# Projections, state-space mixer and out-projection of a hybrid decoder layer, from two staged programs to one unrolled one

## What is computed

```python
proj = rms_norm(x) @ w_in                       # 1024 x (z 1024, x/B/C 1536, dt 16, u 1024, v 1024)
xbc  = silu(causal_conv4(xbc))                  # split: xs 1024, B 2x128, C 2x128
dt   = softplus(dt + dt_bias); a = -exp(a_log)
y, state = ssd_scan(xs, dt, a, B, C, s0, chunk=128)      # 16 heads, state 128
y    = group_rms_norm((y + d_skip * xs) * silu(z)) * ssm_norm_w
u, v = gelu(u), rms_norm(gelu(v)) * sg_norm_w
y_sg = u * (tril(sg_w) @ v + sg_b)              # 8 heads, chunks of 128 rows
h    = x + concat(y, y_sg) @ w_out              # 2048 -> 1024
g    = rms_norm(h)                              # then top-1 of 4 groups, top-2 of 8 experts
h    = h + sum_k gate_k * (silu(g @ Wg[e]) * (g @ Wu[e])) @ Wd[e]
out  = rms_norm(h)
```

## Time and profile before

| | |
|---|---|
| three runs, us | 1735.78, 1738.29, 1739.23 (median 1738.29) |
| span of the profiled execution | 1732.9 us, 23263 instructions |
| its own device time | not listed apart from the span; the median run is 5.4 us above it |
| busy, share of the span | PE 88%, PEld 68%, DVE 63%, ACT 41%, POOL 25% |
| mean granted TensorE clock | 0.922 |
| HBM read, written | 295.30 MB, 55.31 MB |

### The profile page before, as it was taken

The page is one execution under the profiler, slowest core; times in us unless marked ns, Lnnn a source line. Parts: engine busy times, 40 slices in busy tenths (PEclk is TensorE's granted clock), DMA queues, the critical chain, the costliest instruction groups (busy, mean ns, idle before and its releaser), DMA issues. The chain is left out here.

```text
span 1732.9 us, 23263 instructions
## 1 busy us (share of the span) xinstructions
PE 1517.2 (88%) x7338; PEld 1182.8 (68%) x7338; DVE 1099.1 (63%) x1495; ACT 711.1 (41%) x1014; POOL 437.7 (25%) x323
## 2 busy tenths in 40 slices
PE   5999999999958887779898992899999999999950
PEld 4999998999945544445454222678888888878740
DVE  5014786300147656665654435799999999999947
ACT  6222223322112211222122013677777787777723
POOL 6333333222334212221111000153232322212111
PEclk8999999999978988889898586899999999999985
DMA  4223223232553221122211404899999999999947
GB/s 142 75 78 94 74 87 127 74 98 66 204 176 115 94 95 41 53 94 94 94 59 55 144 29 152 300 395 391 378 381 373 380 379 375 376 372 373 358 176 307
DMA packets 139824, 334.82 MB, mean 193 GB/s; under 512 B 17264, under 2 KB 30352, under 8 KB 138480
## 3 DMA queue, kind: packets, MB, share of 16 engines
q1 hardware_dynamic: 123024, 292.06, 46.5%
q0 software_dynamic: 16768, 42.36, 7.0%
HBM read 295.30 MB, written 55.31 MB: 202 GB/s over the span
## 5 line engine op out<-in xcount | busy, mean ns | idle before, releaser
L59 PE MATMUL bank<-xh,wh 128*128 128x352 f32 x864 | 282.2, 327 | 1.9 <-POOL xl L555 1.9
L61 PE MATMUL bank<-xh,wl 128*128 128x352 f32 x864 | 278.0, 322 | 0.0
L60 PE MATMUL bank<-xl,wh 128*128 128x352 f32 x864 | 278.0, 322 | 0.0
L932 PE MATMUL bank<-w_out_ssm,yT 128*128 128x512 f32 (+1 forms) x288 | 140.4, 650 | 52.3 <-ACT yT L1047 52.3
L1528 ACT CAST wg_h<-wg 128x1024 fp32r<-128x1024 f32 x128 | 135.4, 1058 | 113.2 <-DMA wu<-in_w_up 92.4
L1637 DVE TENSOR_TENSOR wg_l<-wg,wg_h 128x1024 fp32r<-128x1024 f32 x128 | 156.3, 1221 | 25.7 <-ACT wu_h L1529 24.4
L59 PEld LDWEIGHTS bank<-xh,wh 128*128 128x128 f32 x864 | 163.0, 189 | 2.4 <-POOL xl L555 2.0
L60 PEld LDWEIGHTS bank<-xl,wh 128*128 128x128 f32 x864 | 163.4, 189 | 0.0
L61 PEld LDWEIGHTS bank<-xh,wl 128*128 128x128 f32 x864 | 162.7, 188 | 0.0
L451 DVE COPY stage<-bank 128x512 f32<-128x512 f32 x52 | 33.5, 686 | 194.9 <-PE bank L243 194.6
L1638 DVE TENSOR_TENSOR wu_l<-wu,wu_h 128x1024 fp32r<-128x1024 f32 x128 | 155.9, 1218 | 0.0
(11 more groups left out here) (315 smaller groups left out, 2973.9 us busy)
## 6 DMA issues: line engine op xcount, KB each, us to landing
wg<-in_w_gate SPq DMA_DIRECT2D x128, 512.0 KB, 6.3
wu<-in_w_up SPq DMA_DIRECT2D x128, 512.0 KB, 11.8
wd<-in_w_down SPq DMA_DIRECT2D x128, 512.0 KB, 12.3
w<-in_w_in_tiles SPq DMA_DIRECT2D x36, 512.0 KB, 3.3
yy<-scratch_picked SPq DMA_DIRECT2D x8, 1024.0 KB, 12.7
scratch_xb<-stage POOLq DMA_DIRECT2D x10, 512.0 KB, 3.9
xb<-scratch_xb SPq DMA_DIRECT2D x8, 640.0 KB, 7.2
scratch_uT<-feat POOLq DMA_DIRECT2D x8, 528.0 KB, 5.4
```

The lines of the kernel that those rows point to most:

```text
L59: nc.tensor.matmul(acc, lh, rh, start=start, stop=False)
L60: nc.tensor.matmul(acc, lh, rl, start=False, stop=False)
L61: return nc.tensor.matmul(acc, ll, rh, start=False, stop=stop)
L932: last = nc.tensor.matmul(bank[6 + n][0:r2, :], yT[:, k, 0:r2], w_out_ssm[:, k, n * 512:(n + 1) * 512], start=False, stop=(k == KT - 1))
```

## The change

`projections` and `mixer` become one function `front` without loops on any engine. Every SBUF tensor has a hand-given offset in one arena, so that tensors of different phases share bytes. What it does, part by part:

1. **Order of the 36 weight tiles:** first x, B and C (12), then z (8), then eight pairs of one v tile and one u tile. The products themselves (`group`, 24 matmuls for one of three banks) are the same.
2. **dt:** the high and low parts of its weights stand side by side as 32 columns (`w_dt_hl`), so 48 matmuls instead of 72, and they run while the input is still being normalised. What follows is done on 128 partitions x 144 instead of 16 x 1056.
3. **State-space work** of prompt tile i is put between the six groups of v tile i and u tile i (`for i in range(NT)`, lines 589 to 663 of the new file). Its y is scaled, turned, multiplied by `ssm_norm_w` and stored to scratch `yT`.
4. **Sample tile:** its chunk work sits between z tiles. The product of C with an old state becomes 8 matmuls of 4 columns on the state of one sequence (line 647), and one sequence is finished in each of the eight pairs.
5. **Out-projection last:** weights are streamed, 16 slices of 512 KB, three times over (48 slices), each cast by ACT and split by POOL. Three token tiles share a slice: 3 tiles x 2 halves x 3 float32r matmuls of 512 columns.
6. **Spatial gating and routing** are spread over the 16 steps of each group of three tiles: gating in steps 1 to 6, and the norm, turning, router and counts of the three tiles of the group before in steps 0 to 14. Those of the last three tiles come behind the last product.

The cores of it, from the diff (the two old functions are taken out whole):

```diff
-            projections(nc, A, S, C, bank)
-            mixer(nc, A, S, C, bank)
+        front(nc, A, S, C, bank)
...
+    z, xbc, u, v = w[:, :COL_X], w[:, COL_X:COL_DT], w[:, COL_U:COL_U + D], w[:, COL_U + D:]
+    pairs = [part[:, i * P:(i + 1) * P] for i in range(NT) for part in (v, u)]
+    columns = np.concatenate([xbc, z, *pairs], axis=1)
...
+            for i in range(NT):
+                group(qV, 0)
...
+                sums((0, 1))
+                group(qV, 1)
+                    turn_y(i - 1, y)
+                group(qV, 2)
+                sums((2, 3))
+                group(qU, 0)
+                turn(qV)
...
+                group(qU, 1)
...
+                group(qU, 2)
...
...
+            for g in range(3):
+                for k in range(16):
+                    n = 16 * g + k
+                    pe.wait_ge(w_split, W_DONE + n + 1)
+                    for a in range(GROUP):
+                        sh, sl = (yTh[a], yTl[a]) if k < 8 else (ysgh[a], ysgl[a])
+                        for half in range(2):
+                            last = split_product(nc, bank[2 * a + half][0:r, :], (sh[:, k % 8, 0:r], sl[:, k % 8, 0:r]),
+                                                 (woh[n % 3][:, s], wol[n % 3][:, s]), start=(k == 0), stop=(k == 15))
```

More of the change, by code:

```diff
@@ L1 @@
+import math
 from contextlib import ExitStack
@@ L133, in projections @@
[L133 to L140, removed]
@@ new lines, in at, with own @@
+        def at(name, offset, shape, dt=F32):
+            return nc.alloc_sbuf_tensor_at(name, shape, dt, offset=base + offset)
+        used = [SMALL_AT]
+        def own(name, shape, dt=F32):
+            t = at(name, used[0], shape, dt)
+            used[0] += -(-4 * math.prod(shape[1:]) // 32) * 32
+            assert used[0] <= ARENA, (name, used[0])
+            return t
+        xin = [at(f"xin{j}", SEG_AT + 4096 * j, [P, D]) for j in range(3)]
+        xn = [at(f"xn{j}", SEG_AT + 12288 + 4096 * j, [P, D]) for j in range(2)]
@@ new lines, in products, with dt_products @@
+            def products(q):
+                for b in range(NB3):
+                    group(q, b)
+            def dt_products(b):
+                pe.wait_ge(w_split, 1)
+                cols = slice(b * TB, (b + 1) * TB)
+                for k in range(KT):
+                    nc.tensor.matmul(bank[3 + b][0:2 * HEADS, 0:TB], w_dt_hl[:, k, :], xh[:, k, cols], start=(k == 0), stop=False)
+                    last = nc.tensor.matmul(bank[3 + b][0:HEADS, 0:TB], w_dt_hl[:, k, 0:HEADS], xl[:, k, cols], start=False, stop=(k == KT - 1))
+                last.then_inc(dt_psum, 1)
@@ L293, in _ @@
-            products(M_END, M_END - 1, 1)
-            turn(M_END - 2 - (M_V - M_C), M_END - 2, 0)
-            turn(M_END - 1 - (M_V - M_C), M_END - 1, 1)
+                        dt_products(b)
+                        group(0, b)
+            products(1)
+            pe.wait_ge(dt_evicted, NB3)
+            pe.wait_ge(x_scaled, 2 * (NT + 1))
+            for t in range(NT + 1):
+                r = rows_of(t)
+                last = nc.tensor.transpose(bank[6][0:r, 32 * t:32 * t + 32], dt_raw[:, rows(t)], C["ident"][0:32, 0:32])
@@ L416, in _ @@
+            for k in range(15):
+                route_steps(2 * GROUP, k)
         @block.vector
@@ new lines, in count, with route_steps @@
+            def count(t):
+                r = rows_of(t)
+                dve.wait_ge(count_psum, t + 1)
+                wait(dve, counted, t)
+                after(nc.vector.tensor_tensor(S["before"][0:r, t, :], bank[7][0:r, 64:64 + E], run[0:r, :], ALU.add))
+                nc.vector.tensor_tensor(run[:], bank[7][:, 96:96 + E], run[:], ALU.add).then_inc(counted, 1)
+            def route_steps(t0, k):
+                if k == 0:
+                    for t in range(t0, t0 + GROUP):
+                        add_x(t)
+                    norm_h(t0)
+                if k == 1:
+                    norm_h(t0 + 1)
+                if k == 4:
+                    route(t0)
+                if k == 5:
+                    norm_h(t0 + 2)
+                if k == 7:
+                    route(t0 + 1)
+                if k == 8:
+                    count(t0)
+                if k == 10:
+                    route(t0 + 2)
+                if k == 11:
+                    count(t0 + 1)
+                if k == 14:
+                    count(t0 + 2)
```

2122 lines of the change are left out of this document (1156 added, 966 removed).

## The result

The changed kernel takes 1614.33 us (four runs, 1612.51 to 1617.76), the kernel before beside it 1738.7: ratio 0.9292, 95% interval 0.9276 to 0.9309. That is 124 us less, where 152 were forecast: the time lies in the range and 28 us above the point. The profiled execution spans 1613.2 us.

What follows compares the result with a forecast made beforehand. PE was taken to bound the projections, DMA the experts, with the mixer PE with holes. Stage terms put the end of the tail at 906 instead of 1058.6, 152 us less: 1738.3 - 152 = 1586 us, range 1560 to 1645.

Steps and rivals of the forecast that it cites:

- the carried 5.4 us of median over span: Whole kernel: the median of the runs was taken to stay 5.4 us above the profiled span, as before.
- signs of being wrong: Pair above 41 us, group above 90, last count over 50 behind last product, or experts' stage differing by over 5.
- Getting started: Start to the end of the first weight tile: dt's matmuls add 6 us, so it ends at 57.
- x/B/C and z tiles: Weight tiles after the first, with turnings, sample chunk work and 2 us for DVE's dt operations: 242.5 us, to 299.5.
- Pairs: Eight pairs of v and u tiles with state-space work: 39.3 us each at full clock, 314.4 in all, to 614.
- The 0.8 us of stall: In each pair, PE waits 0.8 us for the chain from sums to diagonal products, added to 38.5 us of work.
- rival (b): Pairs have a hole: masks shift by one POOL operation, diagonal products start later; 36 us, 1622 in all; chance 0.16.
- Out-projection: Products 196.5 us, gating, turning, routing, waits of 13, sum 247.5, plus 3.5 for things overlooked: ends at 865.
- Rival (a): DVE and ACT set the out-projection's pace: a group lasts 99 us instead of 84, 45 in all, 1631; chance 0.22.
- Rival (d): Slower than before: straight-line code can't be fed to PE; at 40 ns lost a record, 1784 us; chance 0.04.
- Tail: Last product to last count: three tiles left sharing banks and DVE's chain, 41 us (bounds 33 and 50), to 906.
- experts: What follows the tail: untouched by the change and starting from the same state, so no difference was forecast.

Runs made afterwards that it cites:

- the last run: Changed kernel with 4-column matmuls apart, decay inputs behind masks, other buffer, weight slices first, and weight splits on DVE, behind the additions at group changes: 1578.3 us.
- e1: Kernel before the change, with ACT evicting the turned y ahead of the router's first exponential instead of behind it: 1697.7 us, ratio 0.9783.

## Why the prediction was right in kind and 28 us short

The mechanism is the one that was forecast: PE's idle time fell in sum as counted, and the float32r products took the place of the plain ones. Two terms of the sum were too small, the pairs by 13.6 us and the out-projection by 12.9, and the carried 5.4 us of median over span, too large by 4.3, hid a part of it. Of its own signs of being wrong only one showed, a pair above 41 us: the first, with 50.73, while the others took 38.75 to 40.33. A group of the out-projection took 88 us, and the last count came 39.3 us behind the last product.

**Getting started**, 57 forecast, 60.6 measured. Here executions differ: in kernels with the same code up to this point the second turning of a weight tile's output starts between 82.18 and 86.77 us (85.56 in the profile of the change), with a mean clock of the first 60 us between 0.80 and 0.97. So most of the 3.6 us can be this spread; what dt itself costs was not measured.

**x/B/C and z tiles**, 242.5 forecast, 247 measured (60.6 to 307.6). The waits of over 0.3 us are 2.93 (for ACT's eviction, which stands behind ACT's own work on dt, three table loads of 1.28 us and three activations), 1.18 and 0.55. I had booked 2, and for DVE's share of dt, not for ACT's.

**Pairs**, 314.4 forecast, 328 measured. The sum of PE's work, 38.5, was right to 0.25: 38.75. The 0.8 us of stall that I had booked is in no steady pair. The step that failed is the sentence that, as PE has no holes, I take full clock. PE had no holes and lost the clock in four of seven distances, 6.3 us in all. And the first pair differs from the others: rival (b) came true in this one pair, at 12 us where it said 4.5. What was held against that rival, that DVE gets the port between POOL's two operations, was so in the other pairs (longest mask 4.09 us) and not in this one (9.37), and the low clock came on top.

**Out-projection**, 251 forecast, 263.9 measured. Idle time was right (17.9 for 13 + 3.5), though not where I had it: I had named four at the start for y's split, and it was 6.5 for the store of the state. PE's busy time was not right: 234.5 forecast, 244.7 measured, 239.9 in the last run at a clock of 0.99. (One price was a record's length, 1.95 for the gating, where starts give 1.79 (602.74 - 600.95 in e1); that made the forecast 1.4 us too long, not too short.) So about half of the 10 us is the low clock behind waits, and at most 5 are work that my prices missed; the last run has 3.8 us at a clock of 0.56 too, so the parting is rough.

**Rival (a)**, that DVE and ACT set the pace, was wrong as the pace of the changed kernel, where PE has 17.9 us of idle time in 262.65, and right as a cost: with POOL's splits nearly gone the stage is 15 us shorter, a third of the 45 that it said. **Rival (d)** fell: behind the one slow stretch the records of straight-line code stand 0.16 us apart, as in the loops of before. The Trainium skill, Runtime: NRT & Kernel Launch, section Instruction fetch mechanics, says that the engine's sequencer fetches the next block while it executes the current one; the trace agrees, with the same 0.16 and no extra distance, though it does not show the fetching itself.

**Tail**, 41 forecast, 39.3 measured; **experts**, 674 forecast and 674.4 measured. And the median lies 1.1 us above the span, where I had carried 5.4 over from before: 4 us the other way. The terms together: 3.6 + 4.5 + 13.6 + 12.9 - 1.7 = 32.9, less 4.3, is 28.6, the 28 within rounding. That the total is as near as this is luck in part: had the median lain 5.4 us above the span again, it would have been 32.

## What to carry to other kernels

When a plan says that an engine is never idle, ask as well what it is busy with: here 5 us of narrow matmuls cost 1.6 us of clock behind them in four pairs of seven, and a wait of 4 us cost 12. Before a rewriting, try the small edit at the largest wait: on the kernel before it gave 38 of the 124 us, though the low clock moved to the next wait. And when work is freed on one engine, look for the limit right behind it; three products in place of two cost only 9 to 12 us here, because the second limit was that close.

## What the runs showed of the hardware

- PE's clock fell to its lower level (352-column records 0.29 us apart instead of 0.16) without any idle time, behind 3.5 us of 64-column and 1.8 us of 4-column matmuls; with 3.8 us of wide matmuls between the two it did not, in any of seven pairs. It fell in four of seven pairs of one execution and in five of another, so the narrow stretch alone does not decide it.
- A wait of 1.61 us was enough for the lower level behind it (granted clock 0.64 from 618.0 to 627.4, in the kernel before with the eviction first): the diagonal products and the chunk state behind it took 8.69 us instead of 5.37.
- DVE operations on two elements per partition wait for GpSimd: the cast took 2.24 us on average beside weight splits and 0.52 with nearly none.
- One DVE operation can lose as much as two POOL operations in a row last: one mask took 9.37 us beside two of 3.60 in the first pair, where the same mask takes 0.68 alone; beside two of 4.06 in the later pairs the longest took 4.09.
